# An fp32 decoder layer on one core: the MLP in four blocks of 336 tokens and a pair of 368, whose inner layer takes seven block products in place of eight

## The chip, the cores and the metric

The kernel runs on one core of one Trainium2 chip. The metric is the time on the device in microseconds, from the first to the last instruction of the core and what the device adds around it.

## What is computed

One layer of a hybrid decoder, for 2048 prompt tokens and 32 sample tokens (8 sequences of 4), 2080 in all, 1024 channels, fp32 throughout. A projection to 9 groups of 256 columns feeds four mixers (a gated recurrence, a gated convolution, stick-breaking attention, causal pooling); their outputs are joined and projected back. Then comes the MLP, with a layer norm behind each residual sum:

```python
def mixer_layer(x, ...):
    proj = x @ w_in
    ...
    out = jnp.concatenate([ya, yb, yc, yd], axis=-1) @ w_out
def sq_relu_mlp(x, w1, w2):            # w1: 1024 x 4096, w2: 4096 x 1024
    return jnp.square(jax.nn.relu(x @ w1)) @ w2
...
x = layer_norm(ALPHA * x + mix, ln1_g[l], ln1_b[l])
x = layer_norm(ALPHA * x + sq_relu_mlp(x, w_ff1[l], w_ff2[l]), ln2_g[l], ln2_b[l])
```

## The kernel before

Channels lie on the partitions and tokens along the free dimension. fp32 products are made of three matmuls in the fp32r type: a value is split into a rounded high part and the rest, and hi x hi, hi x lo and lo x hi are summed in PSUM (lines 1136 to 1138). ScalarE makes the high parts by a copy, VectorE the low parts by a subtraction.

The program has three parts. The first (to about 480 us) normalises and projects the tokens. The second, which the change rewrites, is a list of steps: `step_at(n)` says what step n is. After 8 "out" and 2 "late" steps come five blocks of 416 tokens with 72 steps each (the last has 64): "up" steps (one tile of 128 inner channels, `x @ w1`), "down" steps (one tile of 128 output channels over a quarter of the inner channels), and in between the 8 "out" steps of the next block, r = 56 to 63 within a block. Each step is 8 x 3 = 24 matmuls over one weight tile of 128 x 1024, which `dense` issues. The third part is the tail, which normalises the last block by rows and stores it.

What sets the order is written out by hand: each engine runs through the same n and does its share in program order, so a wait on an engine holds back all that stands behind it on that engine. In step n

- SyncE issues the load of weight tile n+4 (`load_weights`, into two raw buffers, once VectorE has made the low part of tile n+2);
- ScalarE runs `hidden(n-1)` for an up step (ReLU L1451, square L1453, high part L1455) and `hi_ahead(n+2)` (L1440), for which there are three weight slots;
- VectorE runs `result(n-1)` for out and down steps (L2005, L2012, L2015), `hidden_lo(n-1)` for up steps (L2022) and `lo_ahead(n+2)` (L1995), so a weight tile is ready up to two steps before PE wants it;
- PE has three PSUM banks for the results of steps.

Between these stand: the prompt attention, one unit in each of 144 steps of blocks 0 to 2 (PE scores L932, ScalarE sigmoids L1395 and L1399, a one-column carry copy on GpSimd L2524, VectorE scan L1951, PE transposes L942, and the product with V L963); the sample attention over the paged cache in block 3 (L1014, L1026, L1056, page loads from SyncE and GpSimd); the first layer norm of the next block, along the partitions, in r = 56 to 70 (`norm1_stream`, `norm1_centre`, reciprocal L2170, `norm1_scale` L2175, `norm1_x_lo` L2182); and the second layer norm of the block before, four rows of 104 tokens in r = 1, 2, 4, 6 (`norm2_row`). At the very end `last_tiles` takes the last three down tiles in two token halves of 208, so that `last_rows` can normalise the first two rows beside the second half.

## Time and profile before

| | |
|---|---|
| time, three runs | 2443.44 us median (2442.67 to 2443.89) |
| profiled execution, first to last instruction | 2440.8 us |
| PE busy | 2406.7 us, 13263 matmuls |
| PE weight loads busy | 2331.5 us |
| VectorE, ScalarE, GpSimd busy | 1585.0, 1286.6, 243.0 us |
| DMA | 351.64 MB, mean 144 GB/s |

All rows below are of that one profiled execution, which is 2.6 us shorter than the median of the runs; the difference lies around its instructions. A matmul's length in the profile is its latency; what it costs in a dense stream is the distance from its start to the next start. The same holds for the vector engines, where neighbours overlap by some hundredths to a tenth of a microsecond.

### The profile page before, as it was taken

The page shows a single profiled execution, that of the slowest core. Times are in us where ns is not written, and L with a number is a line of the kernel's source. Part 1 is how long each engine was busy: PE and PEld are TensorE (multiplying, and loading weights), DVE is VectorE, ACT ScalarE, POOL GpSimd, SP SyncE. Part 2 cuts the span into 40 slices and gives each one's busy share as a digit, 9 for nine tenths or more (in the row PEclk, how much of TensorE's full clock was granted, in tenths as well). Part 3 has the DMA queues.
Part 4 walks back from the last instruction along what each step waited for, and adds up shares of the span by engine and source line. Part 5 has one row for each costly group of instructions (what it writes and reads, how often), then busy time and mean ns, then how long its engine had stood idle before and what let it go on. Part 6 is the DMA issues. An engine that isn't in the chain of part 4 may idle for free.

```text
span 2440.8 us, 36724 instructions
## 1 busy us (share of the span) xinstructions
PE 2406.7 (99%) x13263; PEld 2331.5 (96%) x13263; DVE 1585.0 (65%) x2233; ACT 1286.6 (53%) x1982; POOL 243.0 (10%) x527
## 2 busy tenths in 40 slices
PE   7999999999999999999999999999999999999998
PEld 7999999999999999999999999999999999999998
DVE  7635662656777787777788777757655665764335
ACT  5466523555655745656555565554455555444432
POOL 0012320200001100011100111000122130000000
PEclk9999999999999999999999999999999999999999
DMA  8434554534444434444443443333566674343332
GB/s 257 153 108 143 159 174 138 184 111 130 162 134 139 142 110 144 150 129 144 128 124 117 137 141 124 125 122 114 182 187 187 209 234 134 120 136 117 112 118 83
DMA packets 141526, 351.64 MB, mean 144 GB/s; under 512 B 20625, under 2 KB 64146, under 8 KB 141218
## 3 DMA queue, kind: packets, MB, share of 16 engines
q1 hardware_dynamic: 128994, 312.88, 40.6%
q0 software_dynamic: 12352, 36.42, 4.7%
q8 instruction: 106, 1.74, 0.3%
q14 instruction: 74, 0.61, 0.1%
HBM read 300.11 MB, written 49.12 MB: 143 GB/s over the span
## 4 chain that ended last, share of the span: by engine, by line
PE 95%; DVE 2%; ACT 2%; DMA 1%; issue 1%; SPq 0%; DVEq 0%; ACTq 0%
PE PS L1136 22%; PE PS L1138 22%; PE PS L1137 22%; PE PS L874 5%; PE PS L872 5%; PE PS L873 5%; PE PS L942 2%; PE PS L964 1%; PE PS L932 1%; PE PS L963 1%; PE PS L1026 1%; PE PS L933 1%; PE PS L1056 1%; PE PS L1014 1%; PE PS L912 1%
## 5 line engine op out<-in xcount | busy, mean ns | idle before, releaser
L1440 ACT ACTIVATE w_hi_lo<-w_raw 128x1024 fp32r<-128x1024 f32 x240 | 252.7, 1053 | 283.5 <-PE PS L1138 277.3
L1136 PE MATMUL PS<-a_hi,w_hi_lo 128*128 128x416 f32 x1080 | 385.1, 357 | 1.3 <-DVE w_hi_lo L1995 1.3
L1138 PE MATMUL PS<-a_hi,w_hi_lo 128*128 128x416 f32 x1080 | 379.3, 351 | 0.0
L1137 PE MATMUL PS<-a_lo,w_hi_lo 128*128 128x416 f32 x1080 | 378.6, 351 | 0.0
L1995 DVE TENSOR_TENSOR w_hi_lo<-w_raw,w_hi_lo 128x1024 fp32r<-128x1024 f32 x240 | 292.6, 1219 | 58.1 <-ACT w_hi_lo L1440 55.9
L1136 PE MATMUL PS<-h_hi,w_hi_lo 128*128 128x416 f32 x824 | 294.6, 358 | 0.0
L1138 PE MATMUL PS<-h_hi,w_hi_lo 128*128 128x416 f32 x824 | 290.2, 352 | 0.0
L1137 PE MATMUL PS<-h_lo,w_hi_lo 128*128 128x416 f32 x824 | 289.4, 351 | 0.0
L2022 DVE TENSOR_TENSOR h_lo<-h_full,h_hi 128x416 fp32r<-128x416 f32 x160 | 94.6, 592 | 222.9 <-ACT h_hi L1455 222.8
L1136 PEld LDWEIGHTS PS<-a_hi,w_hi_lo 128*128 128x128 f32 x1080 | 203.0, 188 | 4.1 <-DVE w_hi_lo L1995 1.7
L1137 PEld LDWEIGHTS PS<-a_lo,w_hi_lo 128*128 128x128 f32 x1080 | 203.5, 188 | 2.1
L1138 PEld LDWEIGHTS PS<-a_hi,w_hi_lo 128*128 128x128 f32 x1080 | 202.7, 188 | 2.1
L1440 ACT ACTIVATE w_hi_lo_c<-w_raw 128x1024 fp32r<-128x1024 f32 x120 | 126.4, 1053 | 133.8 <-PE PS L1138 128.9
L1451 ACT ACTIVATE h_full<-PS 128x416 f32<-128x416 f32 x160 | 82.3, 514 | 201.9 <-PE PS L1138 195.7
L1136 PE MATMUL PS<-a_hi,w_hi_lo_c 128*128 128x416 f32 x520 | 185.2, 356 | 1.4 <-DVE a_lo L2028 1.2
L1138 PE MATMUL PS<-a_hi,w_hi_lo_c 128*128 128x416 f32 x520 | 183.5, 353 | 0.0
L1137 PE MATMUL PS<-a_lo,w_hi_lo_c 128*128 128x416 f32 x520 | 182.7, 351 | 0.0
L1951 DVE TENSOR_TENSOR_SCAN n_prompt<-n_prompt 128x512 f32<-128x512 f32 (+3 forms) x160 | 178.7, 1117 | 3.5 <-POOL n_prompt L2517 3.3
L1995 DVE TENSOR_TENSOR w_hi_lo_c<-w_raw,w_hi_lo_c 128x1024 fp32r<-128x1024 f32 x120 | 146.3, 1219 | 34.5 <-ACT w_hi_lo_c L1440 33.6
L1137 PEld LDWEIGHTS PS<-h_lo,w_hi_lo 128*128 128x128 f32 x824 | 155.8, 189 | 2.0
L1136 PEld LDWEIGHTS PS<-h_hi,w_hi_lo 128*128 128x128 f32 x824 | 155.4, 189 | 2.0 <-issue 0.4
L1138 PEld LDWEIGHTS PS<-h_hi,w_hi_lo 128*128 128x128 f32 x824 | 155.1, 188 | 1.5
(336 smaller groups left out, 5203.8 us busy)
## 6 DMA issues: line engine op xcount, KB each, us to landing
w_raw<-w_all SPq DMA_DIRECT2D x380, 512.0 KB, 3.5
proj_scratch<-stage SPq DMA_DIRECT2D x70, 208.0 KB, 1.9
k_rows<-kv_out SPq DMA_DIRECT2D x80, 128.0 KB, 4.0
v_hi_lo<-v_scratch SPq DMA_DIRECT2D x40, 256.0 KB, 4.1
x_scratch<-x_full SPq DMA_DIRECT2D x20, 416.0 KB, 2.9
x_residual<-x_scratch SPq DMA_DIRECT2D x5, 1664.0 KB, 7.6
pages<-ck SPq DMA_DIRECT2D x64, 128.0 KB, 2.2
pages<-ck POOLq DMA_DIRECT2D x64, 128.0 KB, 2.5
```

The costliest lines, as they stand in the source:

```text
L872: pe.matmul(out, w_h, x_hi(b)[:, k, :], start=(k == 0), stop=False)
L873: pe.matmul(out, w_h, x_lo(b)[:, k, :], start=False, stop=False)
L874: ins = pe.matmul(out, w_l, x_hi(b)[:, k, :], start=False, stop=(k == KT - 1))
L942: ins = pe.transpose(PS[:, 5 + 2 * (t % 2), j * P:(j + 1) * P], sP[:, t % 3, j * P:(j + 1) * P], ident[:, :])
L1136: pe.matmul(out, w_h, mh_[:, k, :], start=(g == 0), stop=False)
L1137: pe.matmul(out, w_h, ml_[:, k, :], start=False, stop=False)
L1138: ins = pe.matmul(out, w_l, mh_[:, k, :], start=False, stop=(g == KT - 1))
L1440: act.activation(halves(w_hi(n)), raw_halves(n), ACT.Copy).then_inc(s_wh, 1)
L1451: act.activation(hf[:, f % 2, :], PS[:, (N_P + n) % 3, 0:BLK], ACT.Relu).then_inc(s_r, 1)
L1951: dve.tensor_tensor_scan(rev(n_t[:, 0:w]), rev(n_t[:, 0:w]), rev(n_t[:, 0:w]), n_t[:, w:w + 1], ALU.mult, ALU.bypass).then_inc(s_scan2, 1)
L1995: dve.tensor_tensor(halves(w_lo(n)), raw_halves(n), halves(w_hi(n)).bitcast(F32), ALU.subtract).then_inc(s_wl, 1)
L2022: dve.tensor_tensor(hl[:, i, :], hf[:, f % 2, :], hh[:, i, :].bitcast(F32), ALU.subtract).then_inc(s_hl, 1)
```

## The change

The list of steps is cut to four blocks of 336 tokens (`NA`, `MB`), each with 72 steps as before; the second layer norm works on three rows of 112. The last 736 tokens are two halves of 368 (`HB`), "4" and "5". Their out steps both stand in block 3 (r = 56 to 71, 368 columns wide), and so do both their first layer norms, the second one eight steps behind the first; block 3 thus ends with step 79.

Then comes the pair phase. It has 8 chunks of 4 inner tiles; a chunk has two up halves u (two inner tiles each) and one down part. In an up half the product of 2 x 2 blocks (inner tile, half of the 1024 channels, token half) is made with Winograd's form of Strassen's scheme: seven products of 12 matmuls with 368 columns instead of eight. The weight sums (S1 to S4) are made on GpSimd (`w_sums`, four operations of 128 x 512 for an up half), the token sums once before, on VectorE (`b_x_sum`) and GpSimd. The seven products go to three PSUM banks X, Y, Z; partial results are copied out by ScalarE (`b_copy`), added by VectorE (`b_add`), and PE goes on accumulating on top of the bank, after the copy or, for the last product, after the addition. Weights now come in 128 x 512 pieces, in six slots (`RINGW`), each made when the piece six earlier has been used. The down part has 8 weight pieces and 16 products of 12 matmuls; PE starts it when seven of the chunk's eight low parts of hidden values are there (`b_down`). In the last chunk the down part takes the second token half first, and its rows are normalised beside the first half's products; the tail then has three rows of up to 128 tokens. The token halves of the last three tiles (`last_tiles`) are gone.

The core of the diff:

```diff
+def block_at(n):
+
+    b = min((n - PRE) // STEPS_B, NA - 1)
+    return b, n - PRE - STEPS_B * b
+
...
-        return "out", b + 1, 0, r - 56
-    return "down", b, 3, r % 8
+    if r < 64 or (b == NA - 1 and r < 72):
+        return "out", b + 1 + (r - 56) // KT, 0, r % KT
+    return "down", b, 3, r % KT
...
 PRE = KT + 2
-N_STEPS = PRE + NB * STEPS_B - KT
+NA = 4
+MB = 336
+MNR, MROW = 3, 112
+HB = 368
+B0 = NA * MB
+N_STEPS = PRE + NA * STEPS_B + KT
...
+N_CH = FT // 4
+RINGW = 6
+CH_OPS, CH_EVENTS = 22, 30
...
+        def w_source(i):
+
+            o = i % CH_OPS
+            if o < 14:
+                return (raw_part(0), raw_part(1), sc[:, 1, :], sc[:, 0, :], raw_part(2), raw_part(0), raw_part(3))[o % 7]
+            return raw_part((o - 14) % 4)
...
+        def wait_slot(eng, i):
+
+            if i < RINGW:
+                eng.wait_ge(s_step, N_STEPS - 2 + i // 2)
+            else:
+                eng.wait_ge(s_step, N_STEPS + last_event(i - RINGW))
...
+            def b_product(i, out, x_hi, x_lo, first):
+
+                w = w_slot(i)
+                for k in range(4):
+                    w_h, w_l = w[:, k * P:(k + 1) * P], w[:, HALF + k * P:HALF + (k + 1) * P]
+                    pe.matmul(out, w_h, x_hi[:, k, :], start=(first and k == 0), stop=False, skip_group_check=True)
+                    pe.matmul(out, w_h, x_lo[:, k, :], start=False, stop=False, skip_group_check=True)
+                    ins = pe.matmul(out, w_l, x_hi[:, k, :], start=False, stop=(k == 3), skip_group_check=True)
+                ins.then_inc(s_step, 1)
...
+                for o in range(7):
+                    pe.wait_ge(s_wl, WB + up_op(u, o) + 1)
+                    if u == 0 and o == 1:
+                        free_bank(N_STEPS - 2)
+                    if u == 0 and o < 2:
+                        pe.wait_ge(s_xl, (NB + NA) * KT + 4 * o + 4)
+                    elif u == 0:
+                        pe.wait_ge(s_xl, XB_DONE + o - 1)
+                    if o in (2, 4, 5):
+                        pe.wait_ge(s_bcopy, 3 * u + (1, 2, 3)[(2, 4, 5).index(o)])
+                    if o == 6:
+                        pe.wait_ge(s_badd, 3 * u + 2)
+                    out = (X, Y, X, Z, X, Z, X)[o]
+                    if o < 2:
+                        x_h, x_l = ah[:, 4 * o:4 * o + 4, :], al[:, 4 * o:4 * o + 4, :]
+                    else:
+                        x = (xo_t2, xo_t1, xo_t3, xo_b, xo_t4)[o - 2]
+                        x_h, x_l = x[:, 0, :, :], x[:, 1, :, :]
+                    b_product(up_op(u, o), out, x_h, x_l, o in (0, 1, 3))
...
+                    if m:
+                        b_group(c, m, 1, range(4), bank, True, True)
+                        b_group(c, m, 0, range(4), bank + 1, True, True)
+                    else:
+                        pe.wait_ge(s_hl, FB + 8 * c + 7)
+                        b_group(c, m, 0, (0, 1, 2), bank + 1, True, False)
+                        b_group(c, m, 1, (0, 2, 3, 1), bank, True, True)
+                        pe.wait_ge(s_hl, FB + 8 * c + 8)
+                        b_group(c, m, 0, (3,), bank + 1, False, True)
...
+            def b_x_sum(i):
+
+                if i == 0:
+                    dve.wait_ge(s_xfin, (NA + 1) * KT - 4)
+                    dve.tensor_tensor(xs_t1[:, 1, :, :], xr5[:, 0:4, :], xr[:, 0:4, :], ALU.subtract).then_inc(s_bxf, 1)
+                if i == 1:
+                    dve.wait_ge(s_xfin, (NA + 1) * KT)
+                    wait_apart(dve, s_bxf, 1)
+                    dve.tensor_tensor(xs_t2[:, 1, :, :], xr5[:, 4:8, :], xs_t1[:, 1, :, :],
...
+            def b_add(u, o):
+
+                which, bank = {1: (0, 2), 4: (1, 1 - u % 2), 5: (2, 3)}[o]
+                done = 3 * u + which + 1
+                dve.wait_ge(s_step, N_STEPS + up_event(u, o))
+                dve.wait_ge(s_bcopy, 3 * u + (1, 3, 2)[which])
+                h = b_sum(which)
+                dve.tensor_tensor(h, h, PS[:, bank, 0:HB], ALU.add).then_inc(s_badd, 1)
+                wait_apart(dve, s_badd, done)
+                dve.scalar_tensor_tensor(out=h, in0=h, scalar=0.0, in1=h, op0=ALU.max, op1=ALU.mult).then_inc(s_r, 1)
+
+            def h_lo(u, which):
+
+                dve.wait_ge(s_hh, FB + 4 * u + which + 1)
+                dve.tensor_tensor(b_h(bhl, u, which), b_sum(which), b_h(bhh, u, which).bitcast(F32), ALU.subtract).then_inc(s_hl, 1)
...
+                if n == N_STEPS:
+                    b_x_lo(0)
+                    b_x_lo(1)
+                if n >= N_STEPS - 2:
+                    b_lo(2 * (n - N_STEPS + 2))
+                    b_lo(2 * (n - N_STEPS + 2) + 1)
...
+            for u in range(2 * N_CH):
+                for o in range(7):
+                    if o in (1, 4, 5):
+                        b_add(u, o)
+                    if o == 2:
+                        h_lo(u, 0)
+                    if u == 0 and o in (0, 1, 2):
+                        b_x_lo(o + 2)
+                    if o >= 5:
+                        h_lo(u, o - 4)
+                    b_prepare(up_event(u, o))
+                h_lo(u, 3)
...
+            def w_sums(u):
+
+                c, j = divmod(u, 2)
+                for q in (0, 2):
+                    pool.wait_ge(s_brq[q], 16 * (4 * c + j + 1))
+                if u:
+                    pool.wait_ge(s_wl, WB + up_op(u - 1, 3) + 1)
+                pool.tensor_tensor(sc[:, 0, :], raw_part(2), raw_part(3), ALU.add).then_inc(s_bsum, 1)
+                wait_apart(pool, s_bsum, 4 * u + 1)
+                pool.tensor_tensor(sc[:, 1, :], sc[:, 0, :], raw_part(0), ALU.subtract).then_inc(s_bsum, 1)
+                pool.tensor_tensor(raw_part(2), raw_part(0), raw_part(2), ALU.subtract).then_inc(s_bsum, 1)
+                wait_apart(pool, s_bsum, 4 * u + 3)
+                pool.wait_ge(s_wl, WB + up_op(u, 1) + 1)
+                pool.tensor_tensor(raw_part(0), raw_part(1), sc[:, 1, :], ALU.subtract).then_inc(s_bsum, 1)
+
+            for u in range(2 * N_CH):
+                w_sums(u)
+                if u == 0:
+                    pool.wait_ge(s_xfin, (NA + 1) * KT)
+                    pool.tensor_tensor(xs_t3[:, 1, :, :], xr5[:, 4:8, :], xr5[:, 0:4, :], ALU.subtract).then_inc(s_bx3, 1)
```

**VectorE, where the last blocks are normalised.** Before, the end of block 3 (L2175, L2182: scaling and low part of the tokens, L1995: low part of weights, L2015: results):

```order
L2182 SCALAR_TENSOR_TENSOR a_lo<-x_residual,ln_gb,a_hi 128x416 x4
L2015 TENSOR_TENSOR mlp_sum<-mlp_sum,PS 128x416
L1995 TENSOR_TENSOR w_hi_lo_0<-w_raw,w_hi_lo_0 128x2x512
L2182 SCALAR_TENSOR_TENSOR a_lo<-x_residual,ln_gb,a_hi 128x416 x4
L2015 TENSOR_TENSOR mlp_sum<-mlp_sum,PS 128x416
L1995 TENSOR_TENSOR w_hi_lo_1<-w_raw,w_hi_lo_1 128x2x512
L2015 TENSOR_TENSOR mlp_sum<-mlp_sum,PS 128x416
L1995 TENSOR_TENSOR w_hi_lo_c<-w_raw,w_hi_lo_c 128x2x512
L2022 TENSOR_TENSOR h_lo<-h_full,h_hi 128x416
```

Now, steps 77 to 80, the last of block 3 (L2438 results, L2640 low parts of half weights, L2651 to L2660 token sums, L2669 low parts of token sums):

```order
L2438 TENSOR_TENSOR mlp_sum<-mlp_sum,PS 128x336
L2640 TENSOR_TENSOR w_hi_lo_c<-w_raw,w_hi_lo_c 128x512 x2
L2651 TENSOR_TENSOR x1_sum<-x_residual_5,x_residual 128x1472
L2438 TENSOR_TENSOR mlp_sum<-mlp_sum,PS 128x336
L2640 TENSOR_TENSOR w_hi_lo_0<-w_sums,w_hi_lo_0 128x512 x2
L2655 TENSOR_TENSOR x2_sum<-x_residual_5,x1_sum 128x1472
L2660 TENSOR_TENSOR x4_front<-x_residual,x2_sum 128x736
L2660 TENSOR_TENSOR x4_back<-x_residual,x2_sum 128x736
L2438 TENSOR_TENSOR mlp_sum<-mlp_sum,PS 128x336
L2669 TENSOR_TENSOR x2_hi_lo<-x2_sum,x2_hi_lo 128x1472
L2669 TENSOR_TENSOR x1_hi_lo<-x1_sum,x1_hi_lo 128x1472
L2640 TENSOR_TENSOR w_hi_lo_1<-w_raw,w_hi_lo_1 128x512 x2
```

What stood there was the scaling of one block of 416 tokens; now the sums over both halves, 1472 columns each, come behind the scaling of the second half, and the first weights of the pair phase stand between them.

**VectorE, up steps.** Before, in the last block:

```order
L2022 TENSOR_TENSOR h_lo<-h_full,h_hi 128x416
L1995 TENSOR_TENSOR w_hi_lo_0<-w_raw,w_hi_lo_0 128x2x512
L2022 TENSOR_TENSOR h_lo<-h_full,h_hi 128x416
L1995 TENSOR_TENSOR w_hi_lo_1<-w_raw,w_hi_lo_1 128x2x512
L2022 TENSOR_TENSOR h_lo<-h_full,h_hi 128x416
```

Now, an even up half from its third product to its seventh (L2679, L2681: addition of a product and ReLU squared; L2686: low part of hidden values):

```order
L2640 TENSOR_TENSOR w_hi_lo_c<-w_raw,w_hi_lo_c 128x512
L2640 TENSOR_TENSOR w_hi_lo_c<-w_sums,w_hi_lo_c 128x512
L2679 TENSOR_TENSOR b_sums<-b_sums,PS 128x368
L2681 SCALAR_TENSOR_TENSOR b_sums<-b_sums 128x368
L2640 TENSOR_TENSOR w_hi_lo_0<-w_sums,w_hi_lo_0 128x512
L2679 TENSOR_TENSOR b_sums<-b_sums,PS 128x368
L2681 SCALAR_TENSOR_TENSOR b_sums<-b_sums 128x368
L2686 TENSOR_TENSOR b_h_lo<-b_sums,b_h_hi 128x368
L2640 TENSOR_TENSOR w_hi_lo_0<-w_raw,w_hi_lo_0 128x512
```

Two weight pieces that are made from sums of GpSimd (w_sums) now stand ahead of the additions which PE waits for.

**GpSimd, the same half.** It had nothing in these steps before (its last work was the page loads of block 3). Now, the end of one half's sums and the next half's:

```order
L3065 TENSOR_TENSOR w_sums<-w_raw 128x512
L3067 TENSOR_TENSOR w_sums<-w_sums,w_raw 128x512
L3068 TENSOR_TENSOR w_raw<-w_raw 128x512
L3071 TENSOR_TENSOR w_raw<-w_raw,w_sums 128x512
L3065 TENSOR_TENSOR w_sums<-w_raw 128x512
```

These four operations for each of 16 up halves are new, and each stands between a load and ScalarE's high part.

## Rows read from the trace of the kernel before

**Rows 1.** The page: busy time by engine, and the chain that ended last.

```profile
PE 2406.7 (99%) x13263; PEld 2331.5 (96%) x13263; DVE 1585.0 (65%) x2233; ACT 1286.6 (53%) x1982; POOL 243.0 (10%) x527
...
PE 95%; DVE 2%; ACT 2%; DMA 1%; issue 1%; SPq 0%; DVEq 0%; ACTq 0%
```

**Rows 2.** Windows: stretch, length; busy and count of PE, PEld, DVE, ACT, POOL; clock; DMA share; GB/s.

```profile
1273.10:1310.10 37.00, 37.00 (x198) 36.71 (x197) 32.99 (x45) 16.86 (x22) 0.00 (x0) 1.00 0.38 114
1911.20:2014.30 103.10, 103.10 (x632) 95.90 (x631) 63.82 (x62) 62.22 (x78) 30.10 (x56) 1.00 0.70 225
2205.50:2350.50 145.00, 145.00 (x770) 143.84 (x769) 58.13 (x64) 58.10 (x80) 0.00 (x0) 1.00 0.38 116
```

**Rows 3.** Timeline, PE: start, length; matmuls 512, 256, 208 wide and their successors.

```profile
1761.45 1.09 PE L1026 MATMUL PS<-pages_hi_lo,q_windows 128*128 128x512 f32 x4
1762.38 1.03 PE L1014 MATMUL PS<-ident,pages 128*128 128x128 f32 x8
...
1974.12 1.08 PE L1056 MATMUL PS<-pages_hi_lo,wT_sample 128*32 128x256 f32 x8
1975.04 0.35 PE L1136 MATMUL PS<-h_hi,w_hi_lo 128*128 128x416 f32 x1
...
2412.74 0.27 PE L1161 MATMUL PS<-h_lo,w_hi_lo 128*128 128x208 f32 x1
...
2413.85 0.27 PE L1162 MATMUL PS<-h_hi,w_hi_lo 128*128 128x208 f32 x1
```

**Rows 4.** Timeline, VectorE while block 2 is normalised: start, length, operation.

```profile
1290.57 2.75 DVE L2170 RECIPROCAL ln_rstd<-ln_rstd 128x416 f32<-128x416 f32 x1
1293.42 0.59 DVE L2015 TENSOR_TENSOR mlp_sum<-mlp_sum,PS 128x416 f32<-128x416 f32 x1
1293.93 1.22 DVE L1995 TENSOR_TENSOR w_hi_lo<-w_raw,w_hi_lo 128x1024 fp32r<-128x1024 f32 x1
1295.06 2.33 DVE L2175 SCALAR_TENSOR_TENSOR x_residual<-x_residual,ln_gb,ln_rstd 128x416 f32<-128x416 f32 x4
1297.31 0.58 DVE L2015 TENSOR_TENSOR mlp_sum<-mlp_sum,PS 128x416 f32<-128x416 f32 x1
```

**Rows 5.** Timelines, GpSimd and VectorE at the same moments.

```profile
17.54 2.39 POOL L2418 TENSOR_TENSOR w_hi_lo<-w_raw,w_hi_lo 128x1024 fp32r<-128x1024 f32 x1 [16.89 <-DVE w_hi_lo L1696]
...
18.40 1.97 DVE L1743 TENSOR_TENSOR x_early<-x_full,x_early 128x416 fp32r<-128x416 f32 x1 [0.33 <-ACT x_early L1306]
...
613.55 1.20 DVE L1995 TENSOR_TENSOR w_hi_lo<-w_raw,w_hi_lo 128x1024 fp32r<-128x1024 f32 x1
...
613.77 1.03 POOL L2524 COPY n_prompt<-n_prompt 128x1 f32<-128x1 f32 x1 [3.25 <-DVE n_prompt L1951]
```

**Rows 6.** Timelines, ScalarE in an inner-layer step with attention, and the next PE scores.

```profile
617.17 0.52 ACT L1451 ACTIVATE h_full<-PS 128x416 f32<-128x416 f32 x1 [2.73 <-PE PS L1138]
...
618.89 1.04 ACT L1440 ACTIVATE w_hi_lo<-w_raw 128x1024 fp32r<-128x1024 f32 x1
...
620.88 0.69 ACT L1399 ACTIVATE n_prompt<-PS,nbias_h 128x512 f32<-128x512 f32 x1
...
622.41 0.40 PE L932 MATMUL PS<-k_hi_lo,q_hi_lo 128*128 128x512 f32 x1
```

**Rows 7.** The page, DMA issues: queue, count, size, us from issue to landing.

```profile
w_raw<-w_all SPq DMA_DIRECT2D x380, 512.0 KB, 3.5
```

**Rows 8.** Timeline, PE: a stretch in which the matmuls come further apart.

```profile
1746.38 0.55 PE L1136 MATMUL PS<-h_hi,w_hi_lo 128*128 128x416 f32 x1
1746.72 0.55 PE L1137 MATMUL PS<-h_lo,w_hi_lo 128*128 128x416 f32 x1
```

**Rows 9.** Timeline, VectorE in the tail; windows of the last matmuls and what follows.

```profile
2430.04 1.29 DVE L2093 BATCH_NORM_STATS2 bn<-PS 104x6 f32<-104x512 f32 x2
...
2434.80 2.74 DVE L2113 SCALAR_TENSOR_TENSOR nat<-nat,rstd,gb 104x512 f32<-104x512 f32 x4
...
2428.40:2440.80 12.40, 1.08 (x8) 0.83 (x8) 8.79 (x17) 0.20 (x1) 0.00 (x0) 0.63 0.44 134
```

898 lines of the change are left out of this document (614 added, 284 removed).

## The prediction

> **What bounds the kernel now.** I read the page first. PE is busy for 2406.7 of 2440.8 us, and the chain that ended last runs through PE for 95% [rows 1]: the kernel is a stream of matmuls, and its time is their number times the distance from one to the next, plus stalls. Then the windows. In the last block, where no attention runs, 32 steps of 24 matmuls take 145.0 us, 188.8 ns for each one of 416 columns; VectorE is busy for 40% of it. While the next block is normalised, VectorE is busy for 33.0 of 37.0 us, yet PE still goes without a stop [rows 2]. So PE is the bound everywhere, and VectorE is the one that would take over where steps get shorter or VectorE gets more.
>
> **Term 1, the matmuls: -37 us.** What a matmul costs at other widths is read from distances of starts [rows 3]: four of 512 columns in 0.93 us (232.5 ns), eight of 256 in 0.92 us (115 ns). With 188.8 ns for 416 these are 0.454, 0.449 and 0.454 ns a column: proportional. At 208 columns it is 111 ns (ten distances in 1.11 us) or 0.53 a column, so there a floor rules that lies below 115 ns. I take 0.454 ns: 152.5 ns for 336, 167.0 for 368, both well above the floor. Before: 5 blocks x 1728 matmuls (1536 of the MLP, 192 of the out steps), of which the last 72 are split into 144 of 208: 8568 x 0.1888 + 144 x 0.111 = 1633.6 us. After: 4 x 1728 = 6912 of 336, and of 368 the out steps of two halves (384), 16 up halves x 7 x 12 (1344) and 8 chunks x 16 x 12 (1536): 6912 x 0.1525 + 3264 x 0.167 = 1599.2. That saves 34.4; two rows fewer in the second norm and one in block 0's first make some 24 transposes of 0.11 less, 2.6. The other end: if the cost were a line through 208 and 416 columns (0.37 ns a column and 35 ns), after would be 1660 us, a loss of 26; 512 columns would then take 224 ns, not 232.5, so this end gets little weight. A fixed 5 ns in each matmul would put 256 columns at 118 ns and leave 29.
>
> The Trainium skill ("TensorE: Matmul & The Clock Gate", back-to-back issue gap) has N/2.4 + 2.5 ns for a warm matmul, a fixed part that 1464 more matmuls would pay. The rows of this case have 188.8 where it gives 175.8. By it this term would be -28.
>
> **Term 2, the four blocks of 336: 0.** Their steps shrink by 24 x 36.3 ns = 0.87 us while weight work stays. From starts to starts a VectorE operation takes 0.51 us at 416 columns and 1.13 at 1024 [rows 4], that is 0.085 + 0.00102 w: 0.43 at 336, 0.46 at 368, 0.61 at 512, 0.84 at 736, 1.6 at 1472.
> - Normalising (r = 64 to 71): 8 weights 9.0, 16 scalings and low parts at 0.47, 17 plain operations at 0.43, 4 of double width 3.1, reciprocal 2.3: 29 us in 30, with waits on ScalarE up to 4.4 us late in r = 69. Weights are made two steps (7.3 us) ahead, which covers it; with a further 1.4 us of delay it would not.
> - Attention steps: ScalarE's chain from the end of a step to the sigmoids for which the next scores wait is 4.40 us, and PE asks for them 5.24 us after it [rows 6]. After: 4.2 against 4.37. Still covered, by 0.15 us.
> - Weight loads land after 3.5 us [rows 7]; a raw buffer's round (3.5 + 1.05 + 1.2 + 0.5) fits into two steps.
> - The cached pages: 0.70 of the DMA engines at 225 GB/s in the busiest 103 us [rows 2]; the same bytes in 88 us make 0.82. I take +1 (0 to +6).
>
> **Term 3, the entry into the pair phase: +16 us.** From r = 64 of block 3 to the addition that the seventh product waits for, VectorE has, in its own order: 14 whole weights (15.8), 10 half weights (6.1), 42 plain operations of 368 columns (19.3), 24 scalings and low parts (12.2), 8 of 736 (6.7), two reciprocals (4.9, from 2.75 at 416 [rows 4]), 8 results (3.4), token sums and their low parts (12.9), three operations of the first half (1.4): 83 us. PE has 8 x 4.0 + 8 x 3.7 + 1.3 for the means + 6 products x 2.0 = 75. So 8 are missing even if VectorE never waits. Against it works GpSimd: its 128x1024 subtraction took 2.39 us, and a VectorE subtraction that began inside it took 1.97 instead of 0.59, until it was over; a one-column copy of GpSimd took 1.03 and ended with VectorE's 613.55 operation [rows 5]. One waits for the other. Four sums (1.2 each, half of 2.39) and one of 1472 columns (3.4) fall into this stretch, 8.2 us, of which I count 6 that don't hide under waits of VectorE, and 2 for waits on ScalarE. Bounds 8 and 22. PE should be seen waiting before the third product (its token operand) and before the seventh.
>
> The Trainium skill's "SBUF — State Buffer" (who interferes with whom) says the same of two SBUF inputs on VectorE against a reading GpSimd instruction, and the trace agrees (1.97 us). It adds that an instruction with one SBUF input and PSUM, as the additions here, doesn't contend; no row shows that. Were it wrong, term 4 would grow by some 5 us.
>
> **Term 4, the 8 chunks: +12 us.** A chunk is 30 products of 2.0 us. In an even up half, VectorE's queue has the weight made from GpSimd's second sum ahead of the fifth product's addition. The second raw tile can be loaded 3.9 us into the half, lands at 7.4, two sums bring it to 9.9 (10.6 with a VectorE operation between them), the high part to 11.2; the low part waits out the third sum to 12.4, the addition ends at 12.9. PE wants it at 12.05: 0.9 us. In odd halves the sums fall into the down part and disturb nothing, but the down part wants the sixth product's low part: addition, ReLU squared, high part, low part and one weight between, 2.9 us after its end, of which the seventh product covers 2.0 and the matmul's own latency some 0.2: 0.7. Seven halves (the first is in term 3) x 0.9 + 8 x 0.7 = 12. Bounds: 3 (loads land in 2.5 us, sums take 1.0) and 20.
>
> **Term 5, the tail: +5 us.** Before, 12.4 us pass from the last matmul to the end, 7.5 of them VectorE's two rows of statistics and scalings from 2430.04 to 2437.5 [rows 9]. Now it is three rows, 11.5 us; and VectorE is 1.6 us behind when the last product ends, since a row of 4.6 us and three statistics stand before the last result. 1.6 + 0.9 + 11.5 + 3.3 to the landing is 17.3. Bounds +3, +7.
>
> **Term 6, the clock: +1 us.** PE's stalls of up to 5 us at the entry may cost clock: in one place of the trace, matmuls come 0.34 us apart instead of 0.189 for a while [rows 8], the lower of the two levels (1.2 GHz). Bounds 0 and 4.
>
> **Sum.** -37 + 0 + 1 + 16 + 12 + 5 + 1 = -2: 2438.8 us for the profiled execution, and with the 2.6 us around it 2441.4 for the median. That is no change: this kernel can be told from no change from about 0.2% on, 4.9 us. The forecast's own range, with half the bounds, is 2431 to 2452. I give it 0.45, of which 0.16 lie below 2438.6, 0.21 within and 0.08 above 2448.3.
>
> **Rivals.**
> - *The gaps are small* (0.26). Terms 3 to 5 at their lower ends: 8 + 3 + 3, the rest 0: -37 + 14 = -23, 2420. For it: VectorE has waits in which late work can be caught up, and PE runs today without stops at 89% of VectorE. Against it: 83 us in 75 is plain counting.
> - *GpSimd's sums become the pace of the up halves* (0.16), slower. They are 4.8 us in 14, VectorE's operations with two SBUF inputs 7.5 more, so together 12.3 of 14 if they exclude each other [rows 5]. If a half sum takes 1.8 us instead of 1.2, the second sum comes 1.2 us later and each even half loses 3 us and each odd one 1.5: 8 x 4.5 = 36 instead of 12, 2465. It decides from about 1.5 us a sum on.
> - *Attention steps tip over* (0.07), slower. The 0.15 us of cover are gone and each of some 72 up steps loses 0.15: +11, 2452.
> - *A fixed part for each matmul* (0.06), slower: 5 ns in each and 0.442 a column, 153.4 and 167.6 ns. Term 1 falls to -29: 2450. The 115 ns for 256 columns speak against it [rows 3]. The Trainium skill's gap ("TensorE: Matmul & The Clock Gate", back-to-back issue gap) gives the same time within a microsecond.
>
> Faster by over 0.2%: 0.26 + 0.16 = 0.42. Within: 0.21 + 0.03 of the last two = 0.24. Slower: 0.08 + 0.16 + 0.10 = 0.34. The range that should hold it 8 times in 10 reaches from the first rival to near the second, 2421 to 2462.
>
> **What would show it.** Starts 152 to 153 ns apart in the small blocks and 167 in the pair (term 1; 155 or more means a fixed part). The four small blocks without new stalls of PE. PE waiting for VectorE's token low parts and for the fifth product's addition in the first up half, 12 to 20 us in all (term 3). A window of a later chunk of 61.5 to 62.5 us, against 60.1 for 30 products; 64 or more speaks for GpSimd, whose half sums should then last over 1.5 us. 17 us from the last product to the end. I am wrong if PE stalls in the four blocks, or if a chunk takes 60.5 us or less.

## The result and the profile after

The changed kernel takes 2497.28 us (median of four runs, 2495.04 to 2500.82) against 2443.53 us before (2442.67 to 2443.89): a ratio of 1.0222, with a 95% interval from 1.0207 to 1.0236. It is slower by 2.2%. The forecast was 2441.4 us, no change; its range ended at 2462. The profiled execution of the changed kernel spans 2493.4 us, against 2440.8 before; I compare these two, and the forecast's 2438.8 for such a span.

The page of the changed kernel (busy time, GpSimd's and VectorE's among it, and the chain of waits), which answers to [rows 1]:

```profile
PE 2402.5 (96%) x14699; PEld 2330.4 (93%) x14699; DVE 1744.8 (70%) x2616; ACT 1329.5 (53%) x2175; POOL 333.3 (13%) x592
...
PE 75%; DVE 12%; ACT 5%; DMA 3%; issue 2%; POOL 1%; SPq 0%; DVEq 0%; ACTq 0%; POOLq 0%
```

PE issues 1436 more matmuls and is busy for 4 us less. So the work is hardly cheaper, and the span is 53 us longer: PE now stands still. Of the chain that ended last PE held 95% before, now 75%, and VectorE 12%. What PE waited for behind the start of the kernel (engine line, what it waited for: us in total, times, longest):

```profile
...
PE PS L1439 <- DVE b_sums L2679: 11.8, 8, 3.6
PE PS L1439 <- ACT b_sums L2073: 10.6, 3, 9.5
PE PS L1168 <- ACT n_prompt L1729: 9.4, 5, 4.1
PE PS L1374 <- DVE w_hi_lo L2417: 6.6, 2, 3.3
PE PS L1482 <- DVE b_h_lo L2686: 6.0, 7, 0.9
```

L1439 and L1482 are the products of up halves and down parts, L1168 the scores of the prompt attention, L1374 the dense steps. Three places are seen: the chunks (L2679, L2686), the entry (9.5 and 3.6 us at a time), and the attention in the four small blocks, where I had expected nothing. The two waits of L1374 for a weight's low part lie one in the first steps of block 0, which ends at 532.5, and one in block 3, while the second half's tokens are normalised, which ends at 1911.6. The windows show the places apart (stretch, length; busy and count of PE, PEld, DVE, ACT, POOL; clock; DMA share; GB/s):

```profile
884.50:928.20 43.70, 41.14 (x253) 39.34 (x252) 33.79 (x46) 25.66 (x41) 5.73 (x16) 0.96 0.45 149
1160.40:1190.80 30.40, 30.40 (x199) 30.40 (x198) 27.49 (x43) 15.83 (x22) 0.00 (x0) 1.00 0.38 125
1873.70:1976.40 102.70, 82.62 (x467) 80.05 (x465) 95.34 (x127) 50.11 (x77) 16.96 (x9) 0.91 0.26 88
2030.20:2093.20 63.00, 61.01 (x363) 60.34 (x362) 34.63 (x58) 21.39 (x40) 11.09 (x8) 1.00 0.20 67
2475.50:2493.40 17.90, 1.87 (x13) 1.26 (x12) 13.91 (x28) 0.41 (x2) 0.00 (x0) 0.65 0.32 110
```

The first are steps r = 8 to 15 of block 1, with PE short of work and a granted clock of 0.96. The second is the normalising stretch that answers to 1273.1:1310.1 in [rows 2]: VectorE is busy for 27.5 of 30.4 us and PE never waits. The third is the entry, from r = 64 of block 3 to the seventh product: VectorE is busy for 95.3 of 102.7 us. Then one chunk, then the tail.

Against the forecast, stretch by stretch (the ideal time is matmuls by their measured distance, transposes at 0.11 us):

| | forecast | measured | missed by |
|---|---|---|---|
| matmuls (term 1) | -37 | -20 (154.5 ns for 336 columns, 168.1 for 368) | 17 |
| blocks 0 to 3 up to r = 55 (term 2) | +1 | 1323.9 us; 1530.8 before, less 6528 matmuls x 34.3 ns and 28 transposes, is 1303.8: +20 | 19 |
| r = 56 of block 3 to the end of chunk 0 (terms 3, 6, first chunk of 4) | +18 | 190.1 us, ideal 158.4: +32 | 14 |
| chunks 1 to 7 (term 4) | +11 | 445.1 us, ideal 427.6 (7 x 60.5 and 36 transposes in the last): +17 | 6 |
| tail (term 5) | +5 | 17.9 us instead of 12.4: +6 | 1 |

That is 57 us; the miss of the span is 54.6, and the 2.4 us between them are within the rounding of these rows. The part ahead of the first block took 516.2 us in this trace, and up to 520.8 in those of the variants below. For that scatter, since each experiment has one trace, and since runs of the changed kernel differ by up to 0.23%, the experiments are read stretch by stretch.

### The profile page after: what moved, and what is told of

It reads as the page before. It is cut to its first block, busy times and chain, and to the rows that moved or that the text cites. A ratio compares the mean times of both kernels' runs of the same rounds, so it can differ in the third digit from the quotient of the medians.

```text
span 2493.4 us, 40633 instructions
## 1 busy us (share of the span) xinstructions
PE 2402.5 (96%) x14699; PEld 2330.4 (93%) x14699; DVE 1744.8 (70%) x2616; ACT 1329.5 (53%) x2175; POOL 333.3 (13%) x592
## 4 chain that ended last, share of the span: by engine, by line
PE 75%; DVE 12%; ACT 5%; DMA 3%; issue 2%; POOL 1%; SPq 0%; DVEq 0%; ACTq 0%; POOLq 0%
PE PS L1374 11%; PE PS L1376 11%; PE PS L1375 11%; PE PS L1110 5%; PE PS L1108 5%; PE PS L1109 5%; PE PS L1482 3%; PE PS L1484 3%; PE PS L1483 3%; DMA w_raw<-w_all 3%; PE PS L1178 2%; DVE w_hi_lo L2417 2%; PE PS L1439 2%; PE PS L1441 2%; PE PS L1440 2%
## 5 line engine op out<-in xcount | busy, mean ns | idle before, releaser
L1374 PE MATMUL PS<-a_hi,w_hi_lo 128*128 128x336 f32 (+1 forms) x904 | 289.8, 321 | 3.3 <-DVE w_hi_lo L2417 3.3
L1376 PE MATMUL PS<-a_hi,w_hi_lo 128*128 128x336 f32 (+1 forms) x904 | 287.8, 318 | 0.0
L1375 PE MATMUL PS<-a_lo,w_hi_lo 128*128 128x336 f32 (+1 forms) x904 | 287.1, 318 | 0.0
L2417 DVE TENSOR_TENSOR w_hi_lo<-w_raw,w_hi_lo 128x1024 fp32r<-128x1024 f32 x203 | 247.2, 1218 | 52.0 <-ACT w_hi_lo L1770 49.8
L1374 PE MATMUL PS<-h_hi,w_hi_lo 128*128 128x336 f32 x680 | 222.6, 327 | 3.3 <-DVE w_hi_lo L2417 3.3
L1375 PE MATMUL PS<-h_lo,w_hi_lo 128*128 128x336 f32 x680 | 217.9, 321 | 0.0
L1376 PE MATMUL PS<-h_hi,w_hi_lo 128*128 128x336 f32 x680 | 217.7, 320 | 0.0
L1374 PEld LDWEIGHTS PS<-a_hi,w_hi_lo 128*128 128x128 f32 x904 | 170.9, 189 | 4.6 <-DVE w_hi_lo L2417 3.6
L1376 PEld LDWEIGHTS PS<-a_hi,w_hi_lo 128*128 128x128 f32 x904 | 170.3, 188 | 0.0
L1108 PE MATMUL PS<-x_late,w_hi_lo 128*128 128x416 f32 x416 | 151.3, 364 | 0.0
L1110 PE MATMUL PS<-x_late,w_hi_lo 128*128 128x416 f32 x416 | 146.5, 352 | 0.0
L1109 PE MATMUL PS<-x_late,w_hi_lo 128*128 128x416 f32 x416 | 145.1, 349 | 0.0
L1374 PE MATMUL PS<-a_hi,w_hi_lo_c 128*128 128x336 f32 (+1 forms) x440 | 141.2, 321 | 3.7 <-DVE a_lo L2452 3.2
L1376 PE MATMUL PS<-a_hi,w_hi_lo_c 128*128 128x336 f32 (+1 forms) x440 | 139.8, 318 | 0.0
L1375 PE MATMUL PS<-a_lo,w_hi_lo_c 128*128 128x336 f32 (+1 forms) x440 | 139.4, 317 | 0.0
L1374 PEld LDWEIGHTS PS<-h_hi,w_hi_lo 128*128 128x128 f32 x680 | 130.4, 192 | 4.5 <-DVE w_hi_lo L2417 3.6
```

Source lines behind the costliest of these rows:

```text
L1108: pe.matmul(out, w_h, x_hi(b)[:, k, :], start=(k == 0), stop=False)
L1109: pe.matmul(out, w_h, x_lo(b)[:, k, :], start=False, stop=False)
L1110: ins = pe.matmul(out, w_l, x_hi(b)[:, k, :], start=False, stop=(k == KT - 1))
L1374: pe.matmul(out, w_h, mh_[:, k, 0:w], start=(g == 0), stop=False)
L1375: pe.matmul(out, w_h, ml_[:, k, 0:w], start=False, stop=False)
L1376: ins = pe.matmul(out, w_l, mh_[:, k, 0:w], start=False, stop=(g == KT - 1))
```

## Experiments

All times of stretches (us), from the starts of the last matmuls of steps and products in each trace; "chunks" is the typical value of chunks 2 to 5. Each stretch also holds the time for which the granted clock was 0.50 in it, and that differs between traces: in block 1 of the changed kernel the clock was 0.50 from 893.8 to 897.2 us, in chunk_order2 nowhere in block 1, and that is most of the difference between 43.7 and 42.0.

| kernel | r = 8-15 of blocks 1, 2, 3 | block 3, r = 64-79 | chunk 0: even, odd, down | chunks: even, odd, down | span |
|---|---|---|---|---|---|
| changed kernel | 43.7, 46.5, 60.1 | 73.2 | 32.7, 14.1, 36.6 | 15.4, 14.1, 33.4 | 2493.4 |
| thin_sums | 44.0, 47.1, 60.2 | 77.2 | 23.3, 14.1, 36.4 | 14.1, 14.1, 33.4 | 2479.5 |
| entry_order | 44.0, 46.5, 60.3 | 73.5 | 32.2, 14.1, 36.6 | 15.4, 14.1, 33.4 | 2496.0 |
| chunk_order | 43.8, 46.8, 60.0 | 75.2 | 29.6, 15.9, 36.7 | 14.1, 15.5, 33.7 | 2498.3 |
| thin_rows | 39.3, 41.9, 56.7 | 73.9 | 31.8, 14.1, 36.6 | 15.5, 14.1, 33.4 | 2484.5 |
| rows_124 | 41.0, 43.3, 59.3 | 73.1 | 32.8, 15.2, 38.5 | 15.4, 14.1, 33.4 | 2496.4 |
| chunk_order2 | 42.0, 46.6, 60.1 | 73.1 | 32.4, 14.1, 36.8 | 14.1, 14.1, 33.0 | 2480.3 |
| sums_on_vector | 43.6, 46.8, 60.6 | 73.2 | 24.4, 15.9, 37.9 | 14.1, 14.9, 33.0 | 2484.7 |
| combined | 43.5, 45.6, 58.7 | 73.3 | 27.7, 14.3, 36.5 | 14.1, 14.1, 33.0 | 2474.2 |
| combined_thin_rows | 43.5, 44.3, 57.0 | 73.1 | 26.7, 14.1, 36.6 | 14.1, 14.1, 33.0 | 2468.5 |
| thin_token_lows | 43.8, 46.5, 60.0 | 74.0 | 20.5, 14.1, 36.2 | 14.1, 14.1, 33.0 | 2471.9 |
| combined_thin_rows2 | 39.3, 41.9, 58.3 | 72.8 | 28.8, 14.1, 36.2 | 14.1, 14.1, 33.0 | 2471.4 |

### What a matmul costs

```diff
-                out = PS[:, (N_P + n) % 3, 0:BLK]
+                w = BLK
+                if kind in ("up", "down") and b == NB - 1:
+                    w = {("up", 1): 336, ("down", 1): 368, ("up", 2): 256, ("down", 2): 304, ("up", 3): 400}.get((kind, q), BLK)
+                out = PS[:, (N_P + n) % 3, 0:w]
...
-                    pe.matmul(out, w_h, mh_[:, k, :], start=(g == 0), stop=False)
+                    pe.matmul(out, w_h, mh_[:, k, 0:w], start=(g == 0), stop=False)
```

> The kernel before; in its last block, where no attention runs and VectorE is idle for more than half of the time, the steps of five quarters take 336, 368, 256, 304 and 400 of the 416 columns (the rest of the result is left as it was). Theory A (a matmul costs a fixed part and a part for each column, whatever runs beside it): the three paces seen so far, 154.5 ns at 336, 168.1 at 368 and 188.8 at 416, lie on a line of 10.4 ns and 0.429 ns a column; so 336 columns show 154 to 155 ns here too, 368 show 168, 304 show 141, 256 show 120, 400 show 182. Theory B (the cost is proportional, 0.454 ns a column as in the forecast, and the 2 ns more come from the attention, the loads and the vector work beside the small blocks): 152.5, 167.0, 138, 116 and 181.6 ns in this quiet block.

Windows of the steps with 336, 368, 256 and 400 columns, in the kernel before's quiet last block:

```profile
2208.00:2235.00 27.00, 27.00 (x177) 27.00 (x176) 12.09 (x15) 18.00 (x28) 0.00 (x0) 1.00 0.46 136
2238.00:2267.00 29.00, 29.00 (x176) 29.00 (x175) 13.91 (x15) 7.73 (x8) 0.00 (x0) 1.00 0.46 138
2269.00:2290.00 21.00, 21.00 (x179) 21.00 (x179) 12.26 (x14) 17.17 (x28) 0.00 (x0) 1.00 0.49 151
2320.00:2350.00 30.00, 30.00 (x166) 30.00 (x166) 11.67 (x14) 17.31 (x28) 0.00 (x0) 1.00 0.39 118
```

Two of each count lie across an edge, which leaves 154.3, 166.7, 118.6 and 182.9 ns; step by step the medians are 154.3, 166.4, 118.3 and 183.1, with 138.9 for 304 columns. Neither theory holds. 336 columns cost 154.3 ns with VectorE idle for half of the time, so the 2 ns over the forecast are not the company (against B). And 256 cost 118, not 120, so the fixed part isn't 10 ns either (against A). What fits within 1.3 ns is the forecast's fourth rival, 5 ns and 0.442 ns a column (118.1, 139.3, 153.5, 167.6, 181.8, 188.8). At 368 columns the quiet block even lies below the forecast's 167.0, while the pair phase has 168.1: that difference of some 1.7 ns, 5.5 us over 3264 matmuls, is no fixed part, and its cause stays open.

### The chunks

thin_sums lets GpSimd's sums do nothing, but keeps their waits:

```diff
-                pool.tensor_tensor(sc[:, 0, :], raw_part(2), raw_part(3), ALU.add).then_inc(s_bsum, 1)
+                pool.tensor_tensor(sc[:, 0, 0:8], raw_part(2)[:, 0:8], raw_part(3)[:, 0:8], ALU.add).then_inc(s_bsum, 1)
```

(and so the other three sums.)

> The changed kernel without the weight sums: GpSimd's four operations of each up half keep their waits and their place but take 8 columns instead of 512, and the products use raw weights in their place. The token sum on GpSimd stays. Theory A (the second sum on GpSimd is what the seventh product waits for in even halves, by way of VectorE's queue, and GpSimd and VectorE exclude each other): a later chunk takes 61.5 to 61.7 us instead of 62.96, the 1.3 us wait in its even half is gone and the 1.0 us wait at the start of its down part stays; at the entry the wait of 9.6 us before the third product falls to 3 to 6 and the one of 3.7 us before the seventh to under 1; the span falls by 15 to 20 us, to about 2475. Theory B (the landing of the second raw tile and VectorE's own work set the even half): its wait stays at 1 us or more, chunks at 62.6 or more.

The even halves lose their wait to the last tenth (15.4 to 14.1 us), the down part keeps its own, and the first even half gets 9.4 us shorter: its third product waits for 4.4 us, its seventh for under 1. Theory A holds at every place it names. The span fell by only 13.9 us, since r = 64 to 79 of block 3, ahead of the edit, took 4 us more in this run.

How the wait comes about stands in the timelines of an even half of the changed kernel (start, length; idle time before and what ended it):

```profile
2101.55 1.29 POOL L3065 TENSOR_TENSOR w_sums<-w_raw 128x512 f32<-128x512 f32 x1 [21.02 <-DMA w_raw<-w_all]
2102.98 1.29 POOL L3067 TENSOR_TENSOR w_sums<-w_sums,w_raw 128x512 f32<-128x512 f32 x1
2104.23 1.30 POOL L3068 TENSOR_TENSOR w_raw<-w_raw 128x512 f32<-128x512 f32 x1
2105.68 1.54 POOL L3071 TENSOR_TENSOR w_raw<-w_raw,w_sums 128x512 f32<-128x512 f32 x1
...
2104.97 1.11 DVE L2640 TENSOR_TENSOR w_hi_lo<-w_sums,w_hi_lo 128x512 fp32r<-128x512 f32 x1 [3.30 <-ACT w_hi_lo L1791]
2106.01 0.53 DVE L2679 TENSOR_TENSOR b_sums<-b_sums,PS 128x368 f32<-128x368 f32 x1
2106.64 0.98 DVE L2681 SCALAR_TENSOR_TENSOR b_sums<-b_sums 128x368 f32<-128x368 f32 x1
...
2106.68 0.41 PE L1439 MATMUL PS<-x_hi_lo,w_hi_lo 128*128 128x368 f32 x1 [1.16 <-DVE b_sums L2679]
```

The raw tile lands 8.2 us into the half; two sums; then VectorE, which has stood idle for 3.3 us at this weight, makes its low part, 1.11 us long in place of 0.69, since GpSimd's third sum holds it up to 2105.53; only then comes the addition that PE wants. VectorE was not short of time but stood at the wrong wait. So the order should cure it:

```diff
-                    if o in (1, 4, 5):
+                    if o in (1, 5):
                         b_add(u, o)
...
+                    if o == 3:
+                        b_add(u, 4)
```

> The changed kernel; in every up half VectorE adds the fifth product before it makes the low part of the weight piece that stands ahead of it. Theory A (the wait before the seventh product in even halves is the place in VectorE's queue): the 1.3 us are gone in every even half, a later chunk takes 61.6 us instead of 62.96, and of the 3.7 us before the seventh product of the first half 1 to 3 go; the span falls by 10 to 13 us. Theory B (the sums are late whatever the order): the wait moves to the product that uses the second sum and chunks stay at 62.5 or more.

A miss that teaches: the even half is cured (14.1) and the odd one takes the loss over (15.5), and the down part 0.3 more. VectorE and PE at that place in chunk 1:

```profile
2045.28 1.41 DVE L2640 TENSOR_TENSOR w_hi_lo_c<-w_sums,w_hi_lo_c 128x512 fp32r<-128x512 f32 x1 [0.30 <-ACT w_hi_lo_c L1791]
2046.61 1.76 DVE L2640 TENSOR_TENSOR w_hi_lo<-w_sums,w_hi_lo 128x512 fp32r<-128x512 f32 x1
2048.30 0.53 DVE L2679 TENSOR_TENSOR b_sums<-b_sums,PS 128x368 f32<-128x368 f32 x1
...
2048.92 0.41 PE L1439 MATMUL PS<-a_hi,w_hi_lo 128*128 128x368 f32 x1 [1.25 <-issue]
```

The next addition (of the sixth product) stands behind two weight pieces that share their time with GpSimd, and the next half's first product waits for it. (The profile gives no releaser for PE here; the program has `pe.wait_ge(s_badd, 3 * u)` at this place, and the addition ends 0.09 us before PE starts.) Both additions have to go ahead:

```diff
-                    if o in (1, 4, 5):
+                    if o in (1, 5) or (o == 4 and u % 2):
                         b_add(u, o)
...
+                    if o == 3 and u % 2 == 0:
+                        b_add(u, 4)
                     if o >= 5:
                         h_lo(u, o - 4)
-                    b_prepare(up_event(u, o))
+                    late = (5,) if u % 2 else (3, 4, 5)
+                    for e in (late + (6,) if o == 6 else () if o in late else (o,)):
+                        b_prepare(up_event(u, e))
```

> The changed kernel; in an even up half VectorE makes the three weight pieces that come from GpSimd's sums only behind both additions; in an odd half the last low part of hidden values goes ahead of a weight piece. Theory A (all of the chunk's loss is the order in VectorE's queue): even halves 14.1 us instead of 15.4, odd halves stay at 14.1 (they went to 15.5 when only one addition was moved), the down part 33.0 instead of 33.4; a later chunk takes 61.2 us instead of 62.96, the first one loses 2 to 4 less, and the span falls by 12 to 16 us. Theory B (there is too much work for VectorE and GpSimd in a half, whatever the order): the 1.3 us come back in the odd half or in the next product again.

The window of chunk 1, which answers to 2030.20:2093.20 above:

```profile
2030.10:2091.30 61.20, 60.73 (x362) 60.46 (x362) 34.84 (x58) 21.17 (x40) 10.80 (x8) 1.00 0.21 69
```

61.2 us, with the same work on every engine. Theory A holds for the later chunks: all of the loss beyond 0.7 us a chunk was order. It fails for the first chunk, which was to lose 2 to 4 us less: its even half takes 32.4 us, nearly as in the changed kernel, where chunk_order had 29.6.

### The entry

```diff
+                if n == N_STEPS - 1:
+                    b_x_sum(1)
+                    b_x_sum(2)
                 if n >= N_STEPS - 2:
                     b_lo(2 * (n - N_STEPS + 2))
                     b_lo(2 * (n - N_STEPS + 2) + 1)
```

> The changed kernel; in the last step of block 3 VectorE makes the second and third token sum before the low parts of the third and fourth weight piece, not behind them. Theory A (the third product waits for its token operand because VectorE stands 2.9 us at a weight piece that comes from GpSimd's sums, and then shares the time with GpSimd): the wait of 9.6 us before the third product falls to 2 to 5, the span by 5 to 8 us. Theory B (VectorE simply has too much work there, or GpSimd's operations take the time in any order): the wait stays over 8 us or comes back before the next products, and the span changes by less than 2.

The even half took 32.2 instead of 32.7 us: theory B. The timelines say why, first of the changed kernel, then of entry_order:

```profile
1948.87 2.80 DVE L2640 TENSOR_TENSOR w_hi_lo<-w_sums,w_hi_lo 128x512 fp32r<-128x512 f32 x2 [2.87 <-ACT w_hi_lo L1791]
1949.57 1.56 POOL L3071 TENSOR_TENSOR w_raw<-w_raw,w_sums 128x512 f32<-128x512 f32 x1
1951.08 3.73 POOL L3077 TENSOR_TENSOR x_sum<-x_residual 128x1472 f32<-128x1472 f32 x1
1951.60 4.77 DVE L2655 TENSOR_TENSOR x_sum<-x_residual,x_sum 128x1472 f32<-128x1472 f32 x1
```

```profile
1954.73 5.46 DVE L2640 TENSOR_TENSOR w_hi_lo<-w_sums,w_hi_lo 128x512 fp32r<-128x512 f32 x2
...
1955.91 3.73 POOL L3079 TENSOR_TENSOR x_sum<-x_residual 128x1472 f32<-128x1472 f32 x1
```

Whatever VectorE does beside GpSimd's token sum waits for it to end: before, its own token sum took 4.77 us for 1.68; now two weight pieces took 5.46 for 1.3. Another order only changes who pays. So the sums were given to VectorE itself, for all halves:

```diff
-                pool.tensor_tensor(sc[:, 0, :], raw_part(2), raw_part(3), ALU.add).then_inc(s_bsum, 1)
+                dve.tensor_tensor(sc[:, 0, :], raw_part(2), raw_part(3), ALU.add).then_inc(s_bsum, 1)
...
-                    pool.tensor_tensor(xs_t3[:, 1, :, :], xr5[:, 4:8, :], xr5[:, 0:4, :], ALU.subtract).then_inc(s_bx3, 1)
+                    dve.tensor_tensor(xs_t3[:, 1, :, :], xr5[:, 4:8, :], xr5[:, 0:4, :], ALU.subtract).then_inc(s_bx3, 1)
```

> As chunk_order2, and all weight sums and the third token sum are made on VectorE instead of GpSimd (0.69 us for a half sum instead of 1.3 to 2.7; 1.7 us for the token sum instead of 3.7). Theory A (what GpSimd does there stops VectorE for longer than VectorE would need itself): at the entry the wait of 9.6 us before the third product falls to 3 to 6 and the one before the seventh from 3.7 to under 1; chunks stay at 61.2; the span falls by a further 5 to 10 us against chunk_order2. Theory B (GpSimd takes work off VectorE after all): VectorE has 2.8 us more in each half of 14 us, chunks take 62 us or more and the entry gets longer.

Both theories are right, each at a place. The first even half falls from 32.4 to 24.4 us although VectorE has 4.4 us more to do there; its timeline now has the true prices:

```profile
1948.54 0.68 DVE L2643 TENSOR_TENSOR w_sums<-w_raw 128x512 f32<-128x512 f32 x1
...
1952.53 1.68 DVE L2672 TENSOR_TENSOR x_sum<-x_residual,x_sum 128x1472 f32<-128x1472 f32 x1
```

But in the later chunks the odd halves go to 14.9, and the span is 4.4 us above that of chunk_order2: where VectorE waits for the next result anyway, GpSimd does take work off it.

The last test of the entry takes 8 us of VectorE's work away, with the token sums placed as in combined below:

```diff
-                    ins = dve.tensor_tensor(dst[1], src, dst[0].bitcast(F32), ALU.subtract)
+                    ins = dve.tensor_tensor(dst[1][:, :, 0:2], src[:, :, 0:2], dst[0][:, :, 0:2].bitcast(F32), ALU.subtract)
```

> As combined but with ScalarE's order as in the changed kernel, and VectorE makes the low parts of the five token operands for 2 of 368 columns; the products three to seven use the low part of the plain tokens in their place. That takes some 8 us of work from VectorE in the first even half. Theory A (the entry is as long as VectorE's work in it: in the changed kernel VectorE is busy for 95.3 of the 102.7 us from r = 64 of block 3 to the seventh product): the first chunk's even half falls from 27.7 to 20 to 22 us, the wait before the third product from 6.3 to 3 to 5. Theory B (a chain through ScalarE's copies and the loads sets it): less than 3 us of the 8 come back. The steps 8 to 15 of blocks 1 and 2 are back at 43.7 and 46.5 us or below (42 and 46).

The half takes 20.5 us instead of the 27.7 of combined, so 7.2 come back: theory A. In the windows of this half VectorE's busy time falls by 10.2 us, from 26.6 of 27.7 to 16.5 of 20.5, so the half was as long as VectorE's work in combined and is no longer quite so here.

### The attention steps of the small blocks

```diff
+                few = 8 if e < MNR * NA else 512
                 for h in range(2):
-                    ins = dve.bn_stats(bn[0:n, j, h, :], PS[0:n, bank + h, :])
+                    ins = dve.bn_stats(bn[0:n, j, h, :], PS[0:n, bank + h, 0:few])
```

(and the first of the two scalings of a row is left out.)

> The changed kernel; the second norm of blocks 0 to 2 (nine rows) leaves out the mean's subtraction and takes its statistics from 8 of 512 columns, so each row costs VectorE some 2.4 us instead of 5.0. Theory A (the attention steps at the start of blocks 1, 2 and 3 stall because three rows, weights and low parts fill VectorE from r = 1 to 8, 28.8 of 32.1 us, so that it reaches the first attention slot late): the steps 8 to 15 of blocks 1, 2 and 3 take 39.5, 41.5 and 56 us instead of 43.7, 46.5 and 60.1; the span falls by 12 to 14 us. Theory B (these stalls are the landing of weight loads, 3.5 to 4 us, in a ring that the shorter steps leave no time): at most 3 us of the 14 go.

Steps 0 to 7 and 8 to 15 of block 1 in this run, the second to be held against 884.50:928.20 above:

```profile
855.70:887.80 32.10, 32.10 (x219) 32.04 (x217) 21.02 (x37) 21.56 (x40) 0.00 (x0) 1.00 0.57 174
887.80:927.10 39.30, 39.30 (x253) 37.91 (x252) 31.66 (x44) 24.32 (x39) 5.75 (x16) 1.00 0.47 152
```

39.3, 41.9 and 56.7 us: theory A, within 0.7; 12.3 us of the change's loss are the second norm's rows. Not all of that is waiting. In block 1 of the changed kernel PE waits once, for 2.6 us, and then the clock is 0.50 for 3.4 us; in thin_rows both are gone, the granted clock is 1.00 in place of 0.96, and the stretch at 0.50 in block 2 is gone too. By the distances of the matmuls each of the two stretches cost 1.4 us. VectorE, moreover, was not full: it was busy for 25.7 of the 32.1 us of steps 0 to 7 (21.0 in thin_rows), where the expectation had counted 28.8 for r = 1 to 8. The span fell by 8.9, since the part ahead of the first block was 2.6 longer. How a late row reaches PE, in block 2 of the changed kernel:

```profile
1219.32 1.28 DVE L2624 SCALAR_TENSOR_TENSOR nat<-PS,mv,gb 112x1024 f32<-112x1024 f32 x1
1220.71 1.28 DVE L2626 SCALAR_TENSOR_TENSOR nat<-nat,rstd,gb 112x1024 f32<-112x1024 f32 x1
...
1223.94 1.23 DVE L2417 TENSOR_TENSOR w_hi_lo<-w_raw,w_hi_lo 128x1024 fp32r<-128x1024 f32 x1
...
1227.72 1.06 ACT L1770 ACTIVATE w_hi_lo<-w_raw 128x1024 fp32r<-128x1024 f32 x1 [2.32 <-DMA w_raw<-w_all]
1228.69 0.58 ACT L1738 ACTIVATE wT_hi<-PS 128x512 fp32r<-128x512 f32 x1
1229.28 1.28 ACT L1725 ACT_TABLE_LOAD   x1
1230.58 0.69 ACT L1725 ACTIVATE s_prompt<-PS,bias_h 128x512 f32<-128x512 f32 x1
1231.16 0.68 ACT L1729 ACTIVATE n_prompt<-PS,nbias_h 128x512 f32<-128x512 f32 x1
...
1231.90 0.79 PE L1168 MATMUL PS<-k_hi_lo,q_hi_lo 128*128 128x512 f32 x1 [4.15 <-ACT n_prompt L1729]
```

The row makes the weights' low parts late, so SyncE issues the load of the next tile late; ScalarE stands at that tile for 2.3 us with the attention unit behind it, and the unit begins with a load of ScalarE's function table, 1.28 us; PE asks for the unit's sigmoids and waits for 4.15 us. The kernel before has such a table load in each of blocks 0 to 2 as well, and the longest of PE's waits for sigmoids there was 0.7 us. None of the links is long, and I had looked at each alone.

```diff
-ROWS2 = (1, 3, 5)
+ROWS2 = (1, 2, 4)
```

> The changed kernel with the three rows of the second norm in r = 1, 2, 4 of a block instead of 1, 3, 5. Theory A (VectorE has about 29 us of work in the 32 us before the first attention slot and comes to it late because the last row stands only two steps ahead): the same work is done a step earlier, the stalls at the start of blocks 1 to 3 (4.4, 5.1, 4.2 us) halve, the span falls by 4 to 8 us. Theory B (the sum of the work counts, not its place; or weights get late between the rows): no change within 2 us, or a new wait in r = 2 to 4 that costs as much.

Theory B. Steps 8 to 15 fall by 2.7, 3.1 and 0.8 us (in blocks 1 and 2 the clock stays at 1.00, which is 1.4 us each), but steps 0 to 7 rise from 32.1 to 34.0, 33.8 and 34.0, and chunk 0, where the rows of block 3 move too, loses 3 more. The loss moves with the row. That VectorE has too much work in sum is not shown by this: it was busy for 25.7 of 32.1 us.

### Together

combined has chunk_order2, the sums of the first half and the third token sum on VectorE, and ScalarE's attention unit ahead of the weight in four steps:

```diff
+                first = b in (1, 2) and r in (8, 9)
+                if n in SLOT_AT and first:
+                    attention(SLOT_AT[n])
                 if n:
                     hi_ahead(n + 2)
-                if n in SLOT_AT:
+                if n in SLOT_AT and not first:
```

> The changed kernel with the order of chunk_order2, with the first half's weight sums and the third token sum on VectorE (the later halves' sums stay on GpSimd), and with ScalarE taking the attention unit before the weight's high part in the first two attention steps of blocks 1 and 2. Theory A (three separate losses, each cured at its place): chunks 1 to 7 at 61.2 us with odd halves at 14.1; the first chunk's even half 24.4 us as with all sums on VectorE, its odd half and down part back at 14.1 and 36.6; the steps 8 to 15 of blocks 1 and 2 at 41 to 42 and 43 to 44.5 us instead of 43.7 and 46.5; the span falls by 24 to 28 us to 2466 to 2470, still 1.0% to 1.2% slower than before. Theory B (VectorE's work at the entry is too much whatever the place of the sums, and the attention's lateness is VectorE's and not the place in ScalarE's queue): the first chunk keeps 80 us or more, the attention steps do not move or weights get late two steps on; the span stays over 2475.

2476.77 us, 1.0137 times before (1.0118 to 1.0155): 22 of the 54 us of loss are cured by placement alone. It is the best complete version here, and still slower than before. The chunks are as expected; the first even half is 27.7, not 24.4, since, as far as the timeline shows, the second half's sums on GpSimd fall into it (1.4 to 2.0 us each); and the attention steps hardly move: the wait goes from the scores to the transposes behind them.

> As combined, and the nine rows of the second norm of blocks 0 to 2 leave out the mean's subtraction and take statistics from 8 of 512 columns. If the losses add up, the span falls by a further 8 to 12 us, to 2456 to 2460; it stays above the 2440.8 of before, because the matmuls' pace (154.5 and 168.1 ns) leaves only some 20 us of gain and the entry alone costs more than that. If it comes to 2445 or less, the pace is not what limits the change.

Too optimistic by 8 us or more: with thin rows, the steps of block 1 took 43.5 us, where thin_rows alone had 39.3. That pointed at ScalarE's new order:

> As combined_thin_rows, but ScalarE's order as in the changed kernel. With thin rows alone the steps 8 to 15 of block 1 took 39.3 us, with thin rows and ScalarE's attention unit first 43.5. If that order was the cause, they are back at 39.3 and 41.9 us (block 2) here and the span is 2461 to 2464; if it was chance, they stay at 43 and 44.

39.3 and 41.9 are back: that order costs 4.2 and 2.4 us where the rows are thin, 1.4 of the 4.2 by a stretch at a granted clock of 0.50. With the full rows of combined it had gained 0.2 and 0.9. (Its span is nevertheless 2471.4: against combined_thin_rows the part up to r = 7 of block 0 took 5.6 us more, the first even half 2.1 and block 3 1.3.)

## Why the prediction was wrong

**Term 1** had the right form and the wrong price: 152.5 and 167.0 ns for what measured 154.5 and 168.1. It took 0.454 ns a column to be all, and set the fourth rival (a fixed 5 ns, 153.4 and 167.6 ns) at a chance of 0.06 on one row, 115 ns for 256 columns [rows 3]. The quiet block says 118 ns for them, which is what I had written would speak for that rival. Over 10176 matmuls that is 17 us, 14 of them in the small blocks, where the fixed part is the explanation that fits, and 3.6 in the pair, where the quiet block does not bear it out. The Trainium skill ("TensorE: Matmul & The Clock Gate", back-to-back issue gap) has such a fixed part, 2.5 ns, in its formula for a single warm matmul; by it 336 columns would cost 142.5 ns, an estimate that lies 12 below what the trace shows; its form was nearer than mine, its size was not. (The transposes are 32 fewer in all, where the forecast had 24: 1 us the other way.)

**Term 2** failed most: +1 forecast, +20 measured. I had checked attention steps (0.15 us of cover) and the normalising stretch (two steps of lead) each alone, and both checks held: in blocks 0 to 2 each eight steps from r = 16 to 47 take, within 0.4 us, what they took before less the matmuls' part, and 1160.4:1190.8 is without a stop. What I left out is r = 1 to 7, where three rows of 5.0 us stand. I had counted their number and their transposes, not that their 1024 columns don't shrink with the block while the step does. The step of the prediction that failed is thus its check of the wait for the sigmoids: it took a step in the middle of the attention, with 0.15 us of cover, for the first one behind the rows, where PE waits for up to 4.15 us. thin_rows showed 12.3 us of it. The rest is smaller: a wait of 3.3 us for a weight in the first steps of block 0, and products with the cached pages, where PE waits for `z_sample` seven times, 2.7 us in all.

**Term 3** was the right mechanism, mis-sized: VectorE's work at the entry. Forecast 83 us of work, 6 of exclusion, 2 of waits, against 75 of PE. Measured in 102.7 us: 7.4 idle; 95.3 busy, of which some 7.6 are stretching beside GpSimd (4.77 for 1.68, 4.4 for 2.1, 2.01 for 0.93, 1.75 for 0.69), so 88 of work. Against the forecast that is 5 us more of work, 2 of exclusion and 5 of waits. The longest wait was where I said (third product, 9.5 us), and so was the other (seventh, 3.6). The profile ends the first with ScalarE's copy of the first product (L2073), which stood behind the high part of VectorE's late token sum. A third, of 3.3 us for a weight at 1911.6 while the second half is normalised, I had not foreseen, and no experiment was aimed at it.

**Term 4** holds by mechanism at both places, and in size nearly: 1.3 us in an even half for 0.9, 1.0 at the down part for 0.7. The raw tile landed 8.2 us into the half, not 7.4 (4.3 us after its issue, not 3.5 [rows 7]); the sums made up for half of that, the addition ended at 13.2 instead of 12.9, and PE starts 0.14 us behind it. The second rival, GpSimd as the pace, stayed out: its sums take 1.3 to 1.5 us in a chunk, and odd halves are free of waits. Only at the entry it took up to 2.7 a sum.

**Term 5** was right (17.9 for 17.3 us). **Term 6:** the clock does fall, for some 24 matmuls of the first half, behind its two long waits:

```profile
1950.88 0.33 PE L1441 MATMUL PS<-a_hi,w_hi_lo_c 128*128 128x368 f32 x1
1960.69 0.64 PE L1439 MATMUL PS<-x_hi_lo,w_hi_lo 128*128 128x368 f32 x1 [9.47 <-ACT b_sums L2073]
1961.13 0.51 PE L1440 MATMUL PS<-x_hi_lo,w_hi_lo 128*128 128x368 f32 x1
1961.44 0.51 PE L1441 MATMUL PS<-x_hi_lo,w_hi_lo 128*128 128x368 f32 x1
```

After 9.5 us without a matmul the next 15 come 0.307 us apart (the lower of the two levels, 1.2 GHz), and then 0.168 again. Most of this lies beside VectorE's work, which sets the end there, and so inside term 3. But the clock falls in five more stretches, for 3.4 to 6.8 us at a time: from 532.0, 893.8, 1231.8 and 1562.8 us on in the small blocks, and from 1911.0 on in the entry. Three of the seven in all, as windows:

```profile
893.80:897.20 3.40, 3.40 (x12) 3.11 (x13) 2.91 (x4) 2.71 (x5) 0.00 (x0) 0.50 0.21 83
1911.00:1917.80 6.80, 6.17 (x22) 6.18 (x23) 6.45 (x12) 1.74 (x3) 0.00 (x0) 0.50 0.23 77
1955.40:1965.60 10.20, 4.91 (x16) 4.94 (x17) 10.10 (x11) 7.31 (x8) 0.00 (x0) 0.50 0.14 47
```

In all but the one from 1562.8 PE had just stood, or was standing, for 2.6 us or more at one place; ahead of that one it had waited for 1.1 us at most. Adding up by how much the matmuls in the seven stretches come later than at the full clock gives some 11 us, half of them in the small blocks and half in the entry; the kernel before has one such stretch in its stream of matmuls [rows 8], worth 1.4 us. So the cost of the clock was over the bound of 4 that term 6 gave it, and it fell due at nearly every long wait, not at the entry alone. The table by stretches has these 11 us inside its rows; they are not a further miss.

All these errors have one sign: each term was priced at the place where I looked for it, and none for a place where two terms meet. The forecast named two signs by which it would be wrong; the first, "PE stalls in the four blocks", is what happened.

What stays open: an MLP with these blocks and eight plain products was not tried, so the seven products' own share is only an estimate from the paces above: a chunk of 32 products, if PE never waited in it, would be 64.5 us against 62.96, a gain of 1.5 a chunk or 12 in all, and 27 with the order of chunk_order2, before the entry is paid. Open too are the wait at 1911.6 and the 1.7 ns by which 368 columns cost more in the pair than in the quiet block.

## What to carry to other kernels

When steps get shorter, list what doesn't get shorter with them (rows over channels, weights, loads) and hold each piece against the lead of what stands behind it on its engine, not only where the engine looked busiest before. The busy share alone would not have told: VectorE was busy for 27.5 of 30.4 us where PE never waited, and for 25.7 of 32.1 ahead of the waits. And count with each long wait of PE the slower matmuls behind it. An engine that stands in program order at a slow input delays the quick operations behind it; move all of those ahead of it, since moving one hands the loss to the next. And a helper engine that excludes the helped one, as GpSimd does VectorE here, is only of use where the helped one waits anyway.

## What the runs showed of the hardware

- A matmul of fp32r data at the full clock costs 118, 139, 154, 166 to 168, 183, 188.8 ns for 256, 304, 336, 368, 400, 416 columns; at the lower level (1.2 GHz) 368 columns cost 306 to 307 ns, which is 368 cycles and no fixed part.
- GpSimd and VectorE exclude each other in both directions where VectorE reads two operands from SBUF: GpSimd's 128x512 sum takes 1.29 us alone and up to 2.74 beside VectorE's 1472-column sum; VectorE's 0.69 becomes up to 1.76. The addition with one operand in PSUM took 0.53 us at 2106.01 in the middle of a GpSimd sum, the squaring behind it, from SBUF alone, 0.98 instead of 0.54. The Trainium skill ("SBUF — State Buffer", who interferes with whom) says that a VectorE instruction with at most one input in SBUF does not contend with GpSimd, for which the prediction could show no row; now there is one, and the trace agrees.
- In the changed kernel the granted clock was 0.50 for 3.4 to 10.2 us at each of six waits of PE of 2.6 to 9.5 us, and once behind shorter ones. In chunk_order2 it stayed at 1.00 behind a wait of 2.5 us at 895.2.
- In the run of combined_thin_rows2 the profile gave a mean granted clock of 0.93 to 0.95 in every stretch of 400 or 500 us, 0.94 in all, and 0.99 in the other variants of the changed kernel; its dense steps were as fast (30.33 us for r = 64 to 71 of block 1 in all of them).
